# Two 32-byte pads in SBUF, so that the tiles behind them start on multiples of 64 bytes

## What is computed

```python
def conv_ffn(h, w_in, conv_w, conv_b, w_out):
    u = h @ w_in
    u = lax.conv_general_dilated(u, conv_w[:, None, :], window_strides=(1,),
                                 padding=[(CONV_WIDTH - 1, 0)],
                                 dimension_numbers=('NWC', 'WIO', 'NWC'),
                                 feature_group_count=u.shape[-1]) + conv_b
    g, v = jnp.split(u, 2, axis=-1)
    return (jax.nn.silu(g) * v) @ w_out
```

## Time and profile before

| | |
|---|---|
| median of 3 runs | 2435.19 us (2435.01 to 2442.61) |
| the profiled execution | 2433.96 us |
| its span | 2432.2 us |
| TensorE busy | 2280.1 us, 94% of the span |
| TensorE's mean granted clock | 0.967 |
| DVE, ACT, POOL busy | 55%, 36%, 33% |
| DMA packets, share of 16 engines | 25.4% on the large queue |

### The profile page before, as it was taken

One profiled execution on the slowest core, in us unless ns is written; L12 is line 12 of the kernel. 1 busy time (PEld: TensorE's weight loads), 2 busy tenths in 40 slices (PEclk: granted clock), 3 DMA queues, 4 the chain that ended last, 5 costly groups with the idle time before them and its releaser, 6 DMA issues. The chain is left out here.

```text
span 2432.2 us, 32514 instructions
## 1 busy us (share of the span) xinstructions
PE 2280.1 (94%) x11689; PEld 1843.6 (76%) x11689; DVE 1347.5 (55%) x2258; ACT 866.2 (36%) x1355; POOL 792.7 (33%) x378
## 2 busy tenths in 40 slices
PE   5998998899999999999998999999898799999998
PEld 4776996778878888777776888877676557888876
DVE  4487653477721775156465677711597663777601
ACT  3415111443322333234444333322324564333322
POOL 2000000424443444433223344444463004444442
PEclk8999998899999999999999999999999999999999
DMA  3320000313332233322212233233331003233232
GB/s 116 98 78 1 1 1 7 96 52 99 91 104 87 86 103 100 91 73 54 86 44 81 76 103 95 84 95 97 75 92 46 1 3 94 86 95 96 85 99 82
DMA packets 346540, 179.78 MB, mean 74 GB/s; under 512 B 16839, under 2 KB 343618, under 8 KB 346442
## 3 DMA queue, kind: packets, MB, share of 16 engines
q1 hardware_dynamic: 344842, 177.36, 25.4%
q10 hardware_dynamic: 1056, 1.06, 0.2%
q0 software_dynamic: 544, 0.06, 0.0%
HBM read 176.33 MB, written 2.13 MB: 73 GB/s over the span
## 5 line engine op out<-in xcount | busy, mean ns | idle before, releaser
L298 POOL TENSOR_TENSOR wlo<-raw,whi 128x1024 fp32r<-128x1024 f32 (+3 forms) x327 | 744.3, 2281 | 1551.3 <-ACT whi L294 892.6
L311 PE MATMUL banks<-xhi,whi 128*128 128x512 f32 x1536 | 610.8, 398 | 5.1 <-DVE cb L1038 3.9
L312 PE MATMUL banks<-xlo,whi 128*128 128x512 f32 x1536 | 602.0, 392 | 0.0
L313 PE MATMUL banks<-xhi,wlo 128*128 128x512 f32 x1536 | 601.6, 392 | 0.0
L311 PEld LDWEIGHTS banks<-xhi,whi 128*128 128x128 f32 x1536 | 291.3, 190 | 72.8 <-issue 9.1
L312 PEld LDWEIGHTS banks<-xlo,whi 128*128 128x128 f32 x1536 | 291.1, 190 | 63.5 <-issue 3.8
L313 PEld LDWEIGHTS banks<-xhi,wlo 128*128 128x128 f32 x1536 | 290.9, 189 | 61.8
L879 ACT ACTIVATE whi<-raw 128x1024 fp32r<-128x1024 f32 (+1 forms) x216 | 209.8, 981 | 192.1 <-DMA raw<-in_ffn_w_out_dram 89.1
L967 ACT ACTIVATE cb<-banks,conv 128x512 f32<-128x512 f32 x152 | 118.0, 779 | 445.9 <-DVE banks L1027 445.9
L311 PE MATMUL banks<-ghi,whi 128*128 128x512 f32 x608 | 238.8, 393 | 19.8 <-DVE xT L1069 13.8
L312 PE MATMUL banks<-glo,whi 128*128 128x512 f32 x608 | 237.1, 390 | 0.0
(11 more groups left out here) (453 smaller groups left out, 3057.6 us busy)
## 6 DMA issues: line engine op xcount, KB each, us to landing
raw<-in_ffn_w_in_dram SPq DMA_DIRECT2D x88, 512.0 KB, 3.9
raw<-in_w_ffn_up_dram SPq DMA_DIRECT2D x64, 512.0 KB, 4.1
raw<-in_w_ffn_down_dram SPq DMA_DIRECT2D x32, 512.0 KB, 4.4
raw<-in_ev_w_in_dram SPq DMA_DIRECT2D x25, 512.0 KB, 4.0
raw<-in_ffn_w_out_dram SPq DMA_DIRECT2D x32, 384.0 KB, 3.6
raw<-in_ffn_w_out_dram SPq DMA_DIRECT2D x32, 320.0 KB, 3.3
raw<-in_od_w_in_dram SPq DMA_DIRECT2D x20, 512.0 KB, 3.9
raw<-in_w_in_dram SPq DMA_DIRECT2D x19, 512.0 KB, 4.0
```

Source lines behind the costliest of these rows:

```text
L298: return pool.tensor_tensor(wlo[c][:, 0:n, :], raw[b][:, 0:n, :], whi[c][:, 0:n, :].bitcast(F32), ALU.subtract)
L311: pe.matmul(acc, whi[b][:, k, :], hi(k), start=first and k == 0, stop=False)
L312: pe.matmul(acc, whi[b][:, k, :], lo(k), start=False, stop=False)
L313: mm = pe.matmul(acc, wlo[b][:, k, :], hi(k), start=False, stop=last and k == n - 1)
```

## The change

Two tiles of 32 bytes a partition are allocated ahead of the weights' buffers, one on the left side and one on the right. Nothing reads or writes them.

```diff
@@ -213,6 +213,8 @@
+    sb(whole, "left_pad", [P, 8])
+    sb(whole, "right_pad", [P, 8], F32, "right")
     RAW, CUT, AHEAD = 2, 4, 2
     LOADED = RAW + AHEAD
     raw = [sb(whole, f"raw{i}", [P, KD, P]) for i in range(RAW)]
```

## The result

The changed kernel takes 2467.89 us (median of 4 runs, 2458.12 to 2472.73) beside 2438.9 us of the kernel before on the same chip. The ratio is 1.0112 with a 95% interval of 1.0067 to 1.0156: slower by about 29 us. 2464 us were predicted. (The ratios here, with their intervals, are formed over the single runs and can differ a little from the quotient of the two medians.) The profiled execution took 2458.12 us, with a span of 2456.3 us, 24.1 us more than before, and the same mean granted clock of 0.967.

The account below looks back on a forecast made before the run. TensorE streaming its columns was taken to bound the kernel. 2433.96 us profiled + 24 (up stages) + 5 (projections) = 2463 us, plus 1.2 us for the median: 2464 us; range 2388 to 2473, the forecast's own 2457 to 2473.

Parts of the forecast that it names:

- The forecast case: Matmuls reading `xhi`, `xlo` go from distance 0 to 192, pace 226.7 to 233.3 ns; 2464 us, chance 0.42.
- The four up stages, 24 us: Feed-forward up stages: 3648 matmuls reading `xhi`, `xlo`, each 6.67 ns slower, less the few after stops: 24 us.
- The projections, half of 10.9 us: Projections reading `xhi`, `xlo`: 1632 matmuls, at most 10.9 us; half taken, 5 us, because these stages stop often.
- The terms of zero: Allocations, ACT, DVE, POOL, transfers, plain float32 matmuls, down stages and output projections: 0 us each.
- A: All float32r streams: the 64-byte line matters, not distance; one step less each, 2391 us, chance 0.10; more, 0.07.
- B: Line and distance both count: up stages stay 226.7 ns, down stages and output projections 220 ns; 2422 us, chance 0.13.
- C: No effect: 32 and 64 bytes alike, the slower output projection has another cause; 2435 us, chance 0.20.
- D: Distance matters with a longer period, such as 512 bytes; at half a step, +3.3 ns, 2450 us; chance with loss 0.08.
- Depends on how far apart the two are: TensorE's float32r matmuls: pace set by distance of moving tile from weights, 226.7 ns at 0, 233.3 at 192.
- Colliding in a pattern of 64-byte lines: In SBUF, moving stream and weight load collide by 64-byte lines; losses are multiples of 6.67 ns, the time of 64 bytes.

Follow-up runs that it names:

- dist_only: Kernel before plus only a right pad of 64 bytes: feed (`xhi`, `xlo`) at distance 192 from the weights, starts still 32 modulo 64; 2468.74 us, ratio 1.0116.
- aligned_same_distance: Kernel before plus 32 bytes left, 224 right: float32r operands on multiples of 64, all distances modulo 256 as before; 2437.64 us, ratio 1.0006.
- hi_stage_0: Kernel before plus one 64-byte pad ahead of hi2, lo2, hi1, lo1, bringing these four from distance 192 to 0; 2439.85 us, ratio 0.9996.
- the sweep: Kernel with its layers left out: rows of 32 equal matmuls at varied start offsets of moving tile or weights; 226.7 ns at distance 0, 233.1 at 192.

## Why the prediction was right

**The forecast case.** The timeline shows 2.80 us for twelve matmuls in an up stage, 2.72 in a down stage, 430 matmuls for 443 in the window, and ACT and DVE as before; each was named ahead.

**The four up stages, 24 us.** Measured 24.0, stage by stage. Number of matmuls times one step is nearly all there is to it, since PE's longest waits there are the same before and after (3.9 us for DVE, 1.2 us of its own).

**The projections, half of 10.9 us.** This term was too small. The spacings under 245 ns in both profiles grew by 7.6 us, and by the same 7.6 us in dist_only. On the mean they were 228.1 ns before and 233.3 ns after (1485 and 1497 spacings of the 1632), 5.2 ns each. So about 8 us and not 5: what was mis-sized is the share of matmuls in the uneven stretches after stops. I took half; before, 442 of them (27%) had a spacing under 245 ns that was not 226 or 227 ns, and a tenth stood at a stop or at the lower clock. With 8 us the sum is 2467 us; the median measured is 2467.89. The length of these stages as a whole shows it less clearly, because the clock moves them too: the second layer's is 1.9 us shorter in the profile after, and 2.1 us shorter in aligned_same_distance, where no distance had changed.

**What is luck.** The medians differ by 29.0 us, which is the sum of 24 and 5 to the decimal. By the pace it should be 32 us, and the interval of the ratio stands for 16 to 38 us. The measurement of the whole kernel can't tell 29 from 32; only the spacings show that the second term was too small.

**The terms of zero.** Confirmed one by one: ACT 618 ns for 616, DVE 690 for 691, POOL's subtraction for `wlo` 2476 ns for 2483 (L300; the prediction had no row for it), landing 3.7 us for 3.9, the down stages 227.02 ns for 226.95. aligned_same_distance has all of them together, 1.0006 (0.998 to 1.0033). In the third layer's attention one plain float32 group went from 639 to 701 ns. That is two of its 16 instructions at half the pace (lengths of 1216 and 1057 ns for 693 and 589). The same 701 ns stand in hi_stage_0, where nothing of that layer had moved, and 639 in aligned_same_distance, where its operands lie as in the change; so it is not the address.

**The rivals.** A and B ask for alignment to count; aligned_same_distance and the 16 rows of the sweep with both tiles moved exclude that. C asks that the pace of the earlier trace rows have another cause; hi_stage_0 took it away with a pad. D asks for a longer period; 64 rows over 2048 bytes repeat every 256 bytes.

**The mechanism.** "Depends on how far apart the two are" is shown. "Colliding in a pattern of 64-byte lines" is not: distances of 4 bytes matter, and the size of the loss does not follow the number of weight columns. Shown is that the pace belongs to the pair of streams: it moves with either start, with the width of the moving tile and with the number of weight columns, and its dependence on the distance is gone with 16-bit operands (215.8 ns at four distances) and at half the clock (427 ns at distance 0 in the earlier trace rows and at 192 in the kernel after). How the two reads disturb each other inside stays open. The number that carried the forecast, 233.3 ns at distance 192, did not need it; it came from a stage of the same kernel that already lay at that distance.

## What to carry to other kernels

Where TensorE streams float32r back to back, the address of the moving tile relative to the weights, modulo 256 bytes, is worth up to 13 ns in 227 for 128x512 matmuls; that both start on multiples of 64 instead of 32 bytes changed nothing here (1.0006, 0.998 to 1.0033). Any allocation ahead of such tiles, whatever its purpose, can move them: compare (moving - weights) modulo 256 before and after, keep it at 0 for 512 columns, and measure it anew for another width. The pace is seen in twelve neighbouring starts of the timeline, long before it can be told from the spread of the whole kernel's time.

## What was not expected

- Narrower is not always faster, nor is distance 0 always best. 256 columns take 119.9 ns at distance 0 and 113.3 at 192; 488 columns at distance 0 take 225.9 ns and 492 take 222.3.
- Fewer weight columns can cost time: at distance 0, 127 columns take 233.3 ns, 124 take 228.5, 120 take 233.2, and 128 take 226.7.
- 128 moving columns take 111.5 to 111.7 ns at the four distances tried, close to the 113.3 to 119.9 ns of 256.
- A moving tile read at every second word takes 453 ns for 512 columns, twice that of neighbouring words.
- The kernel's run-to-run spread goes with TensorE's granted clock: over 55 runs of the kernel before, from 2423 us to 2447 us, the mean granted clock goes from 0.970 down to 0.959 (correlation -0.96). Where in those runs the clock differs isn't on record; in the profiles of kernels with the same instructions it differs in the first layer's recurrence, 0.50 to 1.00 in the same 20 us.
